# Up projection: 512- and 256-column matmuls in alternation instead of eight and eight

## The reference

```python
D_MODEL, SEQ, D_FF = 2048, 256, 5632
h = rms_norm(x, norm2_w[l]) * (1.0 + sc2) + sh2
u = causal_depthwise_conv(h @ w_up[l], conv_w[l], conv_b[l])   # w_up: (2048, 2 * 5632)
gate, up = u[..., :D_FF], u[..., D_FF:]
x = x + g2 * ((jax.nn.silu(gate) * up) @ w_down[l])
```

## Time and profile before

| | us |
|---|---|
| median of 3 runs | 1318.54 |
| lowest, highest | 1317.94, 1318.63 |
| the profiled execution, its own time | 1316.54 |
| its span, first to last instruction | 1314.7 |
| TensorE busy in the span | 1269.4 (97%) |
| mean granted TensorE clock | 0.982 |

### The profile page before, as it was taken

The page is one execution under the profiler, slowest core; times in us unless marked ns, Lnnn a source line. Parts: engine busy times, 40 slices in busy tenths (PEclk is TensorE's granted clock), DMA queues, the critical chain, the costliest instruction groups (busy, mean ns, idle before and its releaser), DMA issues.

```text
span 1314.7 us, 20785 instructions
## 1 busy us (share of the span) xinstructions
PE 1269.4 (97%) x7298; PEld 1119.3 (85%) x7298; DVE 997.6 (76%) x1278; ACT 608.1 (46%) x793; POOL 51.3 (4%) x99
## 2 busy tenths in 40 slices
PE   4799999999999999989999999999999999999997
PEld 4799999998998878878888888888888878888886
DVE  3788698998888889787878797888777765545454
ACT  3333654444545654454444444444444444434342
POOL 2000000032121000000000000000000000000000
PEclk9788999999999999989999999999999999999999
DMA  9999788888778799749777777777666675555553
GB/s 339 387 385 367 244 299 273 262 275 273 251 254 304 261 341 386 273 152 305 233 240 235 241 226 240 237 238 211 192 189 190 189 259 193 194 195 194 194 195 116
DMA packets 151715, 329.77 MB, mean 251 GB/s; under 512 B 11237, under 2 KB 11990, under 8 KB 150754
## 3 DMA queue, kind: packets, MB, share of 16 engines
q1 hardware_dynamic: 148000, 318.49, 73.1%
q0 software_dynamic: 3360, 9.98, 2.2%
q10 hardware_dynamic: 290, 0.44, 0.1%
HBM read 323.09 MB, written 4.19 MB: 249 GB/s over the span
## 4 chain that ended last, share of the span: by engine, by line
PE 89%; DVE 4%; DMA 3%; ACT 2%; issue 1%; SPq 1%; DVEq 0%; ACTq 0%
PE bank L1182 25%; PE bank L1188 13%; PE bank L1207 6%; PE bank L1209 6%; PE bank L1208 6%; PE bank L943 5%; PE bank L945 5%; PE bank L944 5%; PE bank L930 4%; PE bank L933 4%; PE bank L932 4%; DMA pc<-in_w_ada 3%; DVE acc_c L1323 1%; PE bank L977 1%; PE bank L964 1%
## 5 line engine op out<-in xcount | busy, mean ns | idle before, releaser
L624 ACT ACTIVATE whi<-wraw 128x1024 fp32r<-128x1024 f32 x408 | 432.0, 1060 | 630.1 <-PE bank L1188 238.9
L1311 DVE TENSOR_TENSOR wlo<-wraw,whi 128x1024 fp32r<-128x1024 f32 x404 | 494.0, 1224 | 252.3 <-ACT whi L624 250.8
L1182 PE MATMUL bank<-h,whi 128*128 128x512 f32 x1400 | 351.0, 392 | 0.0
L1182 PEld LDWEIGHTS bank<-h,whi 128*128 128x128 f32 x1400 | 252.2, 189 | 45.2
L1188 PEld LDWEIGHTS bank<-h,wlo 128*128 128x128 f32 x1400 | 191.0, 190 | 13.7
L1188 PE MATMUL bank<-h,wlo 128*128 128x256 f32 x1400 | 195.2, 282 | 0.0
L930 PE MATMUL bank<-h,whi 128*128 128x256 f32 x512 | 149.2, 291 | 3.3 <-DVE h L1336 3.3
L932 PE MATMUL bank<-h,whi 128*128 128x256 f32 x512 | 146.4, 286 | 0.0
L933 PE MATMUL bank<-h,wlo 128*128 128x256 f32 x512 | 146.3, 286 | 0.0
L1207 PE MATMUL bank<-whi,act_hi 128*128 128x512 f32 x336 | 130.8, 389 | 0.3 <-DVE evt L1599 0.3
L1209 PE MATMUL bank<-whi,act_lo 128*128 128x512 f32 x336 | 130.7, 389 | 0.0
(11 more groups left out here) (233 smaller groups left out, 1325.9 us busy)
## 6 DMA issues: line engine op xcount, KB each, us to landing
wraw<-in_w_up SPq DMA_DIRECT2D x176, 512.0 KB, 4.4
araw<-in_w_ada SPq DMA_DIRECT2D x128, 512.0 KB, 5.6
wraw<-in_w_in SPq DMA_DIRECT2D x112, 512.0 KB, 4.9
wraw<-in_w_down SPq DMA_DIRECT2D x88, 512.0 KB, 4.1
pc<-in_w_ada SPq DMA_DIRECT2D x64, 512.0 KB, 11.4
wraw<-in_w_out SPq DMA_DIRECT2D x32, 512.0 KB, 6.0
x<-in_x SPq DMA_DIRECT2D x2, 1024.0 KB, 7.1
x<-in_x POOLq DMA_DIRECT2D x1, 2048.0 KB, 11.4
```

Of the source, the lines that this page charges most:

```text
L624: act.activation(whi[:, slot], wraw[:, slot], ACT.Copy).then_inc(s_hi, 1)
L1182: pe.matmul(ps[bank0 + f], whi[:, slot, k, f * P:(f + 1) * P], h[:, kk].rearrange("p a t -> p (a t)"), start=(kk == 0), stop=False, skip_g ...
L1311: dve.tensor_tensor(wlo[:, slot], wraw[:, slot], whi[:, slot].bitcast(F32), ALU.subtract).then_inc(s_lo, 1)
```

## The change

The eight pairs (f, k) of a unit are put in a list. The loop runs over them with the short matmul one step behind the long one. The wait for s_evac stands ahead of a tile's first long matmul, as before. The wait for s_lo stands ahead of the first short one, which is now the third matmul. In a group's last unit a tile signals after its second short one.

```diff
-                    for f in range(4):
-                        if j == 0:
-                            pe.wait_ge(s_evac, i * 4 + (ph.tile0 + f - reuse + 1 + 4))
-                        for k in range(UK):
+                    order = [(f, k) for f in range(4) for k in range(UK)]
+                    for n in range(len(order) + 1):
+                        if n < len(order):
+                            f, k = order[n]
                             kk = j * UK + k
+                            if j == 0 and k == 0:
+                                pe.wait_ge(s_evac, i * 4 + (ph.tile0 + f - reuse + 1 + 4))
                             pe.matmul(ps[bank0 + f], whi[:, slot, k, f * P:(f + 1) * P], h[:, kk].rearrange("p a t -> p (a t)"),
                                       start=(kk == 0), stop=False, skip_group_check=True)
-                    pe.wait_ge(s_lo, i * ph.units + (ph.unit0 + j + 1))
-                    for f in range(4):
-                        for k in range(UK):
+                        if n == 1:
+                            pe.wait_ge(s_lo, i * ph.units + (ph.unit0 + j + 1))
+                        if n >= 1:
+                            f, k = order[n - 1]
                             kk = j * UK + k
                             last = pe.matmul(ps[bank0 + f][:, 0:SEQ], wlo[:, slot, k, f * P:(f + 1) * P], h[:, kk, 0, :],
                                              start=False, stop=(kk == KT - 1), skip_group_check=True)
-                        if j == ph.units - 1:
-                            last.then_inc(s_pe, 1)
+                            if j == ph.units - 1 and k == UK - 1:
+                                last.then_inc(s_pe, 1)
                     if j < ph.units - 1:
                         last.then_inc(s_pe, 1)
```

## The result

The changed kernel takes 1322.66 us (median of 10 runs, 1321.32 to 1323.18) against 1317.70 of the kernel before (10 runs in the same session). The ratio is 1.0038, with a 95% interval from 1.0030 to 1.0047: **5.0 us slower**. The forecast was 2.1 us faster and called no change and faster equally likely. The direction is wrong. The time lies inside the range only because the range reaches up to the first price of rival B.

What follows compares the result with a forecast made beforehand. The up projection was taken as bound by TensorE's matmul slots: 2781 ns a unit instead of 2793, 12 x 175 = 2.1 us less, so 1318.54 - 2.1 = 1316.4 us. The 8-in-10 range was 1306 to 1325.5.

Steps and rivals of the forecast that it cites:

- rival B: Up projection: short slots in alternation take 120 ns, long ones keep 233.6; +37 ns a unit, 1325.0 us; chance 0.23.
- What bounds the kernel: Up projection, about 490 us: it lasts as long as TensorE's own instruction stream, so only its matmul slots count.
- the wait for wlo: Moves from a unit's ninth matmul to its third; slack falls from 2.98 to 1.6 us, so it costs nothing.
- the banks' waits: Waits for evacuated banks in a group's first unit spread over more of the unit, later than before, and cost nothing.
- the end of the phase: Last evt of ScalarE and VectorE and the down projection's first matmul all come earlier by the sum.
- the choice in the sum: Up projection: a slot depends on the matmul directly ahead, giving 2781 ns a unit, 2.1 us less; chance 0.35.
- the plain sum: Eight long and eight short matmuls of a unit at settled slots: 8 x (226.6 + 120) = 2773 ns.
- the one unit in alternation: Unit at the low clock that already alternates: starts step by 0.64 us without drift or extra; weak support for the forecast.
- Its far end: Up projection: every return from short to long costs the whole 20 ns; 1339.5 us; chance 0.06.
- A: Up projection: alternation settles near 2773 ns a unit or better, 1315.0 us or 1306.5 us; chance 0.33.
- C: First ten units of the up projection: a wlo late by over 1.6 us; 1318 to 1320 us; chance 0.05.
- D: Up projection: the extra over the columns goes altogether, -233 ns a unit, -41 us, 1278 us; chance 0.02.

Runs made afterwards that it cites:

- strict pairs: Against the kernel before, each short matmul directly behind the long one of its own tile and bank, eight pairs a unit: 1323.14 us, ratio 1.0042.
- twos: Against the kernel before, runs of two long and two short matmuls, four of each in a unit: 1316.81 us, ratio 0.9993.
- threes and two: Against the kernel before, runs of three, three and two long matmuls, each followed by as many short ones, in a unit: 1317.47 us in one run.
- fours: Against the kernel before, runs of four long and four short matmuls, two of each in a unit: 1318.95 us, ratio 1.0014.
- eights: The order of the kernel before, eight long then eight short matmuls a unit: 1317.70 us.
- sixteens: Against the kernel before, every other unit does its short matmuls first, giving sixteen long, sixteen short: 1315.77 us, ratio 0.9986.
- thirty-twos: Against the kernel before, units by four, runs of thirty-two: 1315.48 us, ratio 0.9988; only from the third group on, runs of sixteen before: 1314.93 us, 0.9981.

## Why the prediction was wrong, point by point

**What bounds the kernel: right.** The phase is TensorE's stream, nobody waits in it, and the time followed the unit: 26.7 ns x 175 = 4.7 us against 5.0 measured. The counts (175 units, seven alternations) and the wait for wlo, the banks' waits and the end of the phase costing nothing were right too: TensorE's list of waits is empty.

**The step that failed is the choice in the sum**, that a slot depends on the matmul directly ahead. It took 233.6 ns for a long slot behind a short one and 113 for a short one behind a long one, both read at the border of two settled runs. In a settled alternation there is no settled run on either side. In strict pairs the long slots go 233, 241, 236, and the short ones 117, 120, 113. Over the whole phase the means are 236.3 and 117.0: 2.7 ns more for the long, 4 for the short, 6.7 a pair. Seven returns of that are 46.7 ns over the plain sum, where the sum had 8. The border values do occur, once in three. The starts in the trace of the change say the same of its own terms: the seven short slots behind a long one sum to 819 ns where the prediction had 791, the seven long ones behind a short one to 1647 where it had 1635, and the other two are as it had them. So the 113 ns were the larger part of the error.

Strict pairs alone at the full clock would have told it, and the trace of before had none; the one unit in alternation ran at the low clock, and it showed no 13 ns and no excess. I called it weak evidence and yet let it speak.

**The rivals.** B (slower by the short slot, 1325.0, +37 ns a unit) is the nearest, with 26.7. Its pair, 233.6 + 120 = 353.6, has the price of strict pairs (353.3), but not their parts, so that the near sum is in part luck: the short slot averages 117.0, above the break-even of 115 but not 120, and the rest is in the long slot. Its far end, 20 ns at every return, doesn't come: that price needs a long run ahead. A (the excess goes) fails: the unit is 2820, where A had 2773 or 2724, and no long slot of strict pairs is at 226.6. C is seen only when the short matmuls move by several us. D never came near.

**The odds.** Nothing in the rows separated 113 from 120 for a short slot inside an alternation, and the sum stood 1.7 ns a return from break-even (113 against 114.7). With that, 0.35 for the forecast against 0.23 for B was a preference, not a reading.

**Settled and open.** Shown: the excess needs unequal widths, is the same for both patterns of banks tried in runs of eight, and depends on the pattern over several matmuls (three pairs for a round). Per unit it was 53.3 (ones), 46.7 (the change), 13.3 (twos), 23.3 (threes and two), 26.7 (fours), 20 (eights), 10 (sixteens), 5 (thirty-twos). Open: why. Apart from the threes the values are whole multiples of 6.67 ns per round of the pattern (theirs would be over two units), so something inside TensorE seems to fall into step with the stream; that is argued, not shown. No rule that I tried gives the twos. Whether the long ones' loads, which run beside the short matmuls, have a part in it was not tried.

## What to carry to other kernels

Two matmul widths in one stream (512 and 256 columns here) cost time where they meet, and the price inside a tight alternation can't be read off the border of two long runs. Group equal widths into runs as long as the buffers allow, down to one border in thirty-two matmuls here (of the shorter runs, twos were better than eights, and fours worse), and watch that no producer is then wanted too early. When a stream fills its engine, compare whole periods over tens of units in the trace; ten-nanosecond starts are then good to a fraction of one.

## What the hardware showed that I had not expected

- Three settled fp32r slots all fit their columns at 2.4 GHz plus about 0.104 ns for each weight column: 226.7 ns for 512 columns and 120 for 256 with 128 weight columns, 113.3 for 256 with 64. At the low clock a long and a short one take 0.64 us together, without such a part.
- Mixing widths costs 20 ns at a return after a run of eight or more, 13.3 in runs of four, 3.3 in runs of two, 6.7 in strict alternation.
- Strict pairs of 512 and 256 columns never settle: 353.3 ns on average, in rounds of three pairs.
